# Four units of the modulation moved from the first FFN to the first mixer

## The reference, cut to what matters

```
mod = (silu(c) @ w_ada + b_ada).reshape(B, 9, D)     # w_ada: 1024 x 9216
m = [mod[:, j] for j in range(9)]
h = rmsnorm(x, ffn1_pre_g) * (1 + m[1]) + m[0]
x = x + 0.5 * m[2] * rmsnorm(swiglu(h, gate, up, down), ffn1_post_g)
h = rmsnorm(x, mix_pre_g) * (1 + m[4]) + m[3]
proj = h @ w_in                  # q, k, v, q_idx, k_idx, w_idx, x_lru, g_lru
attn = attention over the 64 best keys of each query, chosen by the indexer
lru  = conv(x_lru) -> sigmoid gates -> linear recurrence -> * gelu(g_lru)
x = x + m[5] * rmsnorm(concat(norm(attn), norm(lru)) @ w_out, mix_post_g)
h = rmsnorm(x, ffn2_pre_g) * (1 + m[7]) + m[6]
x = x + 0.5 * m[8] * rmsnorm(swiglu(h, ...), ffn2_post_g)
```

## Time and profile before

| what | value |
|---|---|
| time, median of 3 executions | 2456.57 us (2456.32 to 2457.07) |
| time of the profiled execution | 2458.28 us |
| its span, first to last instruction | 2456.4 us |
| first FFN, on TensorE | 14 us to 210 us |
| first mixer, on TensorE | 218 us to 368 us |
| PE busy | 2416.1 us, 98% of the span |
| DVE busy | 1789.3 us, 73% |
| ACT busy | 1276.7 us, 52% |

### The profile page before, as it was taken

The page is one execution under the profiler, slowest core; times in us unless marked ns, Lnnn a source line. Parts: engine busy times, 40 slices in busy tenths (PEclk is TensorE's granted clock), DMA queues, the critical chain, the costliest instruction groups (busy, mean ns, idle before and its releaser), DMA issues.

```text
span 2456.4 us, 39283 instructions
## 1 busy us (share of the span) xinstructions
PE 2416.1 (98%) x15784; PEld 2101.1 (86%) x15784; DVE 1789.3 (73%) x3466; ACT 1276.7 (52%) x1827; POOL 246.5 (10%) x240
## 2 busy tenths in 40 slices
PE   8999999999999999999999999999999999999999
PEld 8987878988979888888888888988888888888887
DVE  7986666656655788888887556845778888888555
ACT  5545655446564565555444545554565545444454
POOL 0031101002114600000000000212710000000000
PEclk9999999999999999999999999999999999999999
DMA  9897344554335554444545555324455544445554
GB/s 388 314 338 233 121 138 170 214 205 163 121 107 187 180 190 179 172 170 159 180 178 197 199 193 198 122 102 174 172 189 182 178 164 169 168 180 178 206 191 152
DMA packets 73029, 455.77 MB, mean 186 GB/s; under 512 B 9099, under 2 KB 15371, under 8 KB 20754
## 3 DMA queue, kind: packets, MB, share of 16 engines
q1 hardware_dynamic: 72162, 452.21, 51.1%
q0 software_dynamic: 688, 1.06, 0.3%
HBM read 449.17 MB, written 4.06 MB: 185 GB/s over the span
## 4 chain that ended last, share of the span: by engine, by line
PE 90%; DVE 4%; ACT 3%; DMA 1%; issue 1%; POOL 1%; SPq 0%; ACTq 0%; DVEq 0%; POOLq 0%
PE ps L376 19%; PE ps L349 17%; PE ps L351 17%; PE ps L350 17%; PE ps L378 8%; PE ps L2559 2%; PE ps L925 2%; DVE wlo L331 1%; ACT whi L312 1%; PE ps L375 1%; PE ps L395 1%; PE ps L1901 1%; DMA raw<-in_ffn_d 1%; PE ps L1151 1%; PE ps L2539 1%
## 5 line engine op out<-in xcount | busy, mean ns | idle before, releaser
L312 ACT ACTIVATE whi<-raw 128x1024 fp32r<-128x1024 f32 x765 | 809.5, 1060 | 1032.8 <-PE ps L351 639.7
L331 DVE TENSOR_TENSOR wlo<-raw,whi 128x1024 fp32r<-128x1024 f32 x707 | 862.8, 1223 | 516.8 <-ACT whi L312 516.2
L376 PE MATMUL ps<-HT,whi 128*128 128x512 f32 x2048 | 718.6, 399 | 0.0
L378 PE MATMUL ps<-HT,wlo 128*128 128x256 f32 x1792 | 502.1, 280 | 0.0
L376 PEld LDWEIGHTS ps<-HT,whi 128*128 128x128 f32 x2048 | 372.2, 188 | 68.8
L349 PE MATMUL ps<-whi,CT 128*128 128x512 f32 x1024 | 404.0, 395 | 1.2 <-DVE wlo L331 0.9
L350 PE MATMUL ps<-wlo,CT 128*128 128x512 f32 x1024 | 398.7, 389 | 0.0
L351 PE MATMUL ps<-whi,CT 128*128 128x512 f32 x1024 | 398.6, 389 | 0.0
L378 PEld LDWEIGHTS ps<-HT,wlo 128*128 128x128 f32 x1792 | 338.5, 189 | 8.6
L349 PE MATMUL ps<-HT,whi 128*128 128x256 f32 x968 | 278.0, 287 | 2.4 <-DVE wlo L331 1.5
L350 PE MATMUL ps<-HT,whi 128*128 128x256 f32 x968 | 274.6, 284 | 0.0
(11 more groups left out here) (397 smaller groups left out, 3268.8 us busy)
## 6 DMA issues: line engine op xcount, KB each, us to landing
raw<-in_down SPq DMA_DIRECT2D x128, 1024.0 KB, 4.8
raw<-in_up SPq DMA_DIRECT2D x128, 1024.0 KB, 4.8
raw<-in_w_in SPq DMA_DIRECT2D x41, 1024.0 KB, 4.8
raw<-in_ffn_gu SPq DMA_DIRECT2D x36, 1024.0 KB, 4.9
raw<-in_w_ada SPq DMA_DIRECT2D x28, 1024.0 KB, 6.4
raw<-in_ffn_d SPq DMA_DIRECT2D x22, 1024.0 KB, 5.4
raw<-in_w_out SPq DMA_DIRECT2D x12, 1024.0 KB, 4.8
raw<-in_w_ada SPq DMA_DIRECT2D x16, 512.0 KB, 15.7
```

The costliest lines, as they stand in the source:

```text
L312: e.activation(self.whi[:, i % NSPLIT, :], self.raw_of(i), ACT.Copy, bias=0.0, scale=1.0).then_inc(*k.inc("w_hi", ("hi", i)))
L331: e.tensor_tensor(self.wlo[:, n, :], self.raw_of(i), self.whi[:, n, :].bitcast(F32), ALU.subtract).then_inc(*k.inc("w_lo_pool" if pool els ...
L376: t = e.matmul(out.rearrange("p (a t) -> p a t", a=2), hi[:, s], self.HT[:, c, :, :], start=c == 0, stop=c == 7)
L378: t = e.matmul(out[:, 0:T], lo[:, s], self.HH[:, c, :], start=False, stop=False)
```

## The change

Four of the ada units that stood in the first FFN stand in the first mixer: two fewer lie among the gate and up weights, two fewer among the down weights, three more among `w_in`, and one more among `w_out`. Since 59 instead of 63 units then come before `w_in`, the ring of three begins at unit 52 instead of 56, and SyncE issues 63 instead of 67 units ahead of the mixer's own transfers. Counted from the start of `w_in` that is the same place of the stream: three units of `w_in` and one more, which was unit 3 of `w_in` and is now an ada unit.

Three of the units in `w_in` (behind its units 2, 3 and 5) are listed in `self.own`. `lo` passes them by, and VectorE works them off by halves at the end of rounds 2 and 3, 4 and 5, 8 and 9 of the mixer. The unit behind `w_in`'s unit 12 and the two in `w_out` are worked off in `lo` as before.

```
-        mixed(i["ffn1_gu"][8:], 8, [1, 3] + list(range(4, 14)))
-        mixed(i["ffn1_d"], 20, list(range(10)))
-        mixed(i["w_in"], 30, [12], True)
-        mixed(i["w_out"], 31, [1])
+        mixed(i["ffn1_gu"][8:], 8, [1, 3, 4, 5, 6, 8, 9, 10, 12, 13])
+        mixed(i["ffn1_d"], 18, [0, 1, 2, 4, 5, 7, 8, 9])
+        first = len(self.units)
+        mixed(i["w_in"], 26, [2, 3, 5, 12], True)
+
+        self.own = [first + 3, first + 5, first + 8]
+        mixed(i["w_out"], 30, [0, 1])
...
-            turns, n = (ring, u - 56) if u >= 56 else (more, u - 16) if u >= 16 else \
+            turns, n = (ring, u - 52) if u >= 52 else (more, u - 16) if u >= 16 else \
...
+    def passed(self, e, upto):
+        while self.n_unit < upto:
+            if self.kinds[self.n_unit] == "ada" and self.n_unit not in self.own:
+                self.ada(e, self.n_unit)
+            self.n_unit += 1
+
+    def ada(self, e, u, which=(0, 1)):
...
+        def modulation(r):
+            for n, a in {2: ((0, 0),), 3: ((0, 1),), 4: ((1, 0),), 5: ((1, 1),), 8: ((2, 0),), 9: ((2, 1),)}.get(r, ()):
+                self.ada(e, self.own[n], (a,))
...
             proj(r)
+            modulation(r)
...
-        self.load(e, 67)
+        self.load(e, 63)
```

More of the change, by code:

```diff
@@ L322, in lo @@
             u = self.slots[i][0]
[L323 to L326, removed]
+            if not pool:
+                self.passed(e, u)
             if (i in ON_POOL) == pool:
@@ L333, in lo @@
             self.n_lo += 1
-    def ada(self, e, u):
+    def passed(self, e, upto):
[4 more added lines that the diff above has]
+    def ada(self, e, u, which=(0, 1)):
         k, raw = self.k, self.raw[self.place[u]]
-        for a in range(2):
+        for a in which:
             n = ADA[self.ada_at[u] + a]
@@ L865, in opening_dve @@
         for c in range(8):
[L866 to L869, removed]
+            self.passed(e, 2 * c + 1)
             for w in k.late(("ada", 8 + c)):
```

## The result

The changed kernel takes 2459.91 us (median of 18 runs, 2456.83 to 2464.85) where the kernel before, on the same chip, takes 2456.44 (18 runs, 2454.71 to 2459.11). The ratio is 1.0014 [1.0007, 1.002]: slower by 3.5 us, between 1.7 and 4.9. That is inside the 0.2% that I called "same", and inside the range; the forecast of 2457.2 is 2.7 us too low. I had also written that less than 0.2% can't be told from none. Here it can: 0.14%, with an interval that lies wholly above 1. The profiled execution took 2461.32 us around a span of 2459.4, 3.0 us longer than the span before.

The account below looks back on a forecast made before the run. PE, busy 98% of the span, was taken as the bound, so only its waits could be won. A gain of 1.5 and a loss of 2.17 us made +0.65, giving 2457.2 us from the median of 2456.57; range 2453.4 to 2460.0.

Parts of the forecast that it names:

- The gain, -1.5: First FFN, down projection: with two ada units fewer ahead, PE waits go; 1.5 us won, bounds 0 to 1.5.
- The two waits: PE waits at the first down matmul (1.0 us) and for DVE's gate (0.5 us), both forecast to go.
- the third wait: PE wait at 203.78, end of the FFN, forecast to stay: gain 0, at most 1.6 us.
- the backlog: FFN loads some 11.4 us behind by the down projection; two ada units fewer were to take off 6.5 us.
- Rival E: The change does not lighten the FFN, its backlog being made before the skipped units: +2.2 us, 2458.7; chance 0.11.
- Unit 3, slot 72, the ada unit: Mixer: unit 3 lands at 236.4, slot 72's rounding is 3.3 us late, the ada unit's buffer is free at 242.2.
- Rival A: The load behind the bias tiles lands in time or the copies don't reach PE; only the gain remains: 2455.0, chance 0.20.
- Unit 4 in 4.8 us: Mixer: unit 4 leaves at 242.2, lands at 247.05 and delays round 6's gates; PE loses 2.17 us, bounds 0 to 4.2.
- Rival D: Round 6's stall passes 4.04 us and takes the clock down there too: +5.8 us, 2462.4; chance 0.07.
- my case for a clock that falls behind the short stall: If round 6's new stall of some 2 us brought the clock down, the forecast would be +2.9 us, 2459.4.
- Rival B: Round 18: a shift of the 4.04 us wait may end the low clock behind it, worth 2 us: 2455.2, chance 0.12.
- A and B together: Part of the case, with C (the late FFN loads profit too), put at 2451.4 and outside the range; chance 0.05.

Follow-up runs that it names:

- e7: The kernel before, unedited, traced in a second execution: 2456.57 us (1 run), with its first mixer matmul at 216.34.
- e6: The kernel before without the second of GpSimd's two stores of repeated bias rows (384 KB): 2454.95 us, ratio 0.9993 to the kernel before.
- e1: The changed kernel with the three ada units among `w_in` one unit later, so unit 3 loads first: 2455.48 us, ratio 0.9995 to the kernel before.
- e8: The changed kernel with 16 identity matmuls in front of the gates of round 6: 2459.72 us, ratio 1.0012 to the kernel before.
- e5: The changed kernel with 28 identity matmuls in front of the gates of round 6: 2461.80 us, ratio 1.0022 to the kernel before.
- e4: The changed kernel with unit 5 of `w_in` issued only when unit 4 has landed: 2459.28 us, ratio 1.0013 to the kernel before.
- e2: The changed kernel with both halves of the first ada unit in round 2: 2458.25 us, ratio 1.0005 to the kernel before.
- e3: The changed kernel with the eight bias tile transfers issued behind unit 6 of `w_in`: 2459.58 us (1 run).
- e9: e1's kernel with 16 identity matmuls at the head of mixer round 18: 2453.94 us, ratio 0.9987 to the kernel before.
- e10: The kernel before with 16 identity matmuls at the head of mixer round 18: 2454.78 us, ratio 0.9991 to the kernel before.

## Why the prediction was right in its bound and low in its size

**The gain, -1.5: right.** The two waits went for the reason given, with the relief of the queue; against the trace of e7 it is 1.33 us. That the third wait would stay was wrong in the changed kernel's execution, and by the spacing of the earlier trace rows it should have stayed. What the argument lacked is that the wait is not a property of the kernel: e7 doesn't have it with the same order of loads. Leaving it out of the sum was right by luck, not for the reason I gave.

**What the backlog is: half right.** I took it for the sum of the loads ahead. Some 7.2 us of it come with one store on another queue (e6). The relief by two units was still large enough: the first unit of down weights landed 9.6 us sooner, for the 6.5 I had. Rival E fell with this.

**Unit 3, slot 72, the ada unit: right, to the tenth.** 7.7 us behind the tiles, landing at 236.4 and ada done at 242.2 in the old positions. (PE's wait for `QI` was 0.16 us for my 0.35.) Rival A fell: e1 shows that the load was the whole of it.

**Unit 4 in 4.8 us: this term was too small.** I wrote that it goes out "on a queue that is empty by then". Nothing was on its way, but the next load in the list was ready as well: unit 5's buffer came free with `wlo` of slot 73, 1.2 us before unit 4's, and it stood behind unit 4 only because SyncE issues loads in order. The wait that held unit 4 had held unit 5 too, and both left within 0.4 us. 7.0 us for 4.8 made the term 4.37 us for 2.17. It was not always so much: by e8's 6.2 and e5's 5.2 us, with the gates 1.57 us behind the convolution, the term is 3.6 and 2.9 us. Where unit 5 comes later unit 4 takes 4.9 us (e4 and e2, with waits of 1.80 and 0.66). That it is unit 5 which lengthens the transfer stays an inference, with e3's 4.7 us against it.

**The clock: missing from the forecast, present in a rival.** Rival D had this course: unit 4 lands at 249 or later, a stall of 4.1 us, a low clock of 2.2 us and a second late convolution of 1.0. It landed at 249.25 in the same positions, the stall is 3.99 us, the low clock took 1.57, and the convolutions of rounds 8 and 10 were in time. I gave it 0.07, and the reason against it ("nothing lies in the queue at 242") overlooked the load right behind. What is refuted is that it takes a wait of 4.04 us: in e4 the clock fell behind one of 1.80. I had read the earlier trace rows as if 2.36 us always left it at 1.00; e7, the same kernel, has the same wait with the clock down behind it. The Trainium skill's rule ("TensorE: Matmul & The Clock Gate", Part 1: throttled is the default state, and activity releases it) was my case for a clock that falls behind the short stall, at 2459.4; the row of e4 agrees with it, and so does e7's 2.36 us, while the same wait in the first trace of before doesn't.

**Rival B, the fall in round 18 goes: no.** The wait in the changed kernel is again 4.04 us (300.41). The low stretch behind it is about half as long in this trace, and other stretches were low instead. Its price of 2 us was right, as e9 and e10 show with 1.8.

**The rest** came as said: no wait in rounds 8 and 10 at the gates, nothing at slot 93, nothing for the halves on DVE.

**The sum.** -1.33 + 4.37 + 1.57 = +4.6 for an execution like the profiled one, in which unit 4 takes 7.0 us and the clock falls behind the gates, +3.0 for one in which the clock doesn't fall, and +1.5 if unit 4 takes 5.2 us as well; the median of 18 is +3.5. The forecast was +0.65. The difference is 0.7 to 2.2 us at unit 4's transfer and, in an unknown part of the executions, 1.6 us of clock. The range held, but one line about it was wrong: A and B together come to 2453.0, which is below 2453.4.

## What to carry to other kernels

When a load is delayed, ask which loads behind it in the same queue have their buffers free already: they will leave with it, and the transfer that is now urgent may take longer than it does alone (here 4.7 to 7.0 us for 4.8). When one profile shows a short wait, a short transfer or a clock that stays up, take a second execution before it goes into a sum. And where a stall of a few microseconds can't be removed, matmuls that fit into it keep the clock up; measure what one takes first, since too many cost more than the clock (e5).

## What I had not expected of the hardware

- A store of 384 KB from GpSimd's queue took 15.4 us, and with it a load of 1 MB on another queue took 7.2 us longer (16.4 and 9.2 us, e7 and e6).
- Of two loads of 1 MB issued 0.4 us apart, the first landed after 7.0, 6.2, 5.2 and 4.7 us (changed, e8, e5, e3), the second after 9.1, 8.3, 8.4 and 8.2; with 1.15 us between them the first took 4.9 (e2).
- The clock fell behind a wait of 1.80 us (e4), and behind one of 2.36 it fell in one execution of the kernel before (e7) and not in the other. The length of the wait alone doesn't decide; what else does, these runs leave open.
- An identity matmul of 128 columns in fp32 takes 0.22 us from start to start (28 in 6.3 us).
